# Gated recurrent mixer of a three-layer kernel: the order of scores, wide slabs, gate slabs and state rounds, and which engine splits the wide slabs

## The chip, the cores and the metric

The kernel runs on one core of a Trainium2 chip. The metric is device time in microseconds (us), the median of three runs. TensorE, VectorE (DVE), ScalarE (ACT), GpSimd (POOL) and the DMA queue of SyncE (SP) each run an instruction stream of their own; semaphores order them.

## The reference, cut to what matters

Three layers follow each other: a pooling and retention mixer, a gated recurrent mixer (`mixer_c`, stage "c" of the kernel) and a state space mixer, each followed by a routed expert layer ("peer"). The change is in stage c alone. There are 256 tokens of width 1024, eight heads of 128, and chunks of 32 tokens:

```python
def hgrn2_chunkwise(q, k, v, logf):
    b = jnp.cumsum(lc, axis=3)                     # within a chunk of 32
    b_last = b[:, :, :, -1:, :]
    q_in = qc * jnp.exp(b)
    k_in = kc * jnp.exp(-b)
    k_out = kc * jnp.exp(b_last - b)
    scores = jnp.where(causal, jnp.einsum('nbhcd,nbhsd->nbhcs', q_in, k_in), 0.0)
    intra = jnp.einsum('nbhcs,nbhse->nbhce', scores, vc)
    chunk_decay = jnp.exp(b_last[:, :, :, 0, :])
    def step(state, inp):
        cross = jnp.einsum('bhcd,bhde->bhce', q_n, state)
        state = state * d_n[..., None] + jnp.einsum('bhsd,bhse->bhde', k_n, v_n)
        return state, cross

def mixer_c(x, w_in, lower_bound, norm_g, w_out):
    q, fz, i, g = jnp.split(x @ w_in, C_SPLITS, axis=-1)
    f = lower_bound + (1.0 - lower_bound) * jax.nn.sigmoid(fz)
    o = hgrn2_chunkwise(q, 1.0 - f, i, jnp.log(f))
    y = head_rmsnorm(o, norm_g) * jax.nn.silu(g)
    return y @ w_out
```

## The kernel before

All weights stream through a ring of three slots as slabs of 128 x 1024 fp32 (512 KB). A float32 product is made of three matmuls (lines 576 to 578) from two halves of each operand. So each slab passes four steps: SyncE's queue loads it into `ring` (line 375) when the split of the slab three before it is done; ScalarE copies it rounded to `w_hi` (line 829, a "lead") when TensorE has used the slab three before it; GpSimd, or in some stages VectorE, subtracts it to `w_lo` (line 527, `split_rest`, a "split"); TensorE multiplies. `hi`, `lo`, `used` and `evac` count these steps.

Stage c has 40 slabs, numbered here from 0. Slabs 0 to 15 are columns (24 matmuls each, one PSUM bank of 256 columns): the gate logits f of the eight heads, then q. Slabs 16 to 23 are the wide ones (12 matmuls of 512 columns each), which accumulate v over all eight slabs in the four `acc` banks. Slabs 24 to 31 are columns again, the output gate g. Slabs 32 to 39 are rows of the output matrix (12 matmuls each, accumulating in `acc`). A column's PSUM bank is emptied by ScalarE (`column`, line 836, counted by `evac`), which then leads the slab three further on.

Between them lies the recurrence. VectorE turns sigmoid(f) into f (line 1935) and 1 - f (line 1939); ScalarE takes the log of the halves (line 1856); VectorE does the cumulative sums, one scan for each head (line 1943); ScalarE takes exponentials (line 1860), VectorE multiplies them into keys and queries (lines 1951 to 1958). TensorE then makes the scores (line 1774, in `acc`, after v has been copied out at line 849), VectorE masks them into `probs` (line 1962), TensorE transposes the outgoing keys (line 1784, in `acc`), ScalarE copies them (line 1891). Then come four state rounds, for tile 0 and 1 of the tokens and four heads each: `outers` (line 1802) makes the additions to the state of three or four chunks, VectorE folds them into the states (lines 1992 and 1995), `cross` (line 1812) reads the states. `intra` (line 1791) multiplies scores and v. ScalarE squares each tile (line 1898), VectorE and ScalarE make 1/std and y (lines 1969 to 1976), TensorE transposes y (line 1836), VectorE multiplies by gain and gate (line 2006) and halves the result (`coef`, lines 1235 and 1237), and the row slabs follow.

TensorE's order before: slabs 0 to 23; gate slabs 0 and 1 (slabs 24, 25); scores; gate slabs 2 and 3; key transposes; gate slab 4; outers 0, intra 0, gate 5, outers 1, cross 0, gate 6, outers 2, cross 1, intra 1, gate 7, outers 3, cross 2, cross 3; transposes of y; the eight row slabs. GpSimd splits every slab of the stage. Orders are written out by hand for each engine; nothing is planned at run time.

## Time and profile before

| | |
|---|---|
| runs | 2933.29 us median (2929.36 to 2934.74) |
| profiled execution: own time / span | 2932.74 us / 2930.9 us |
| TensorE busy | 2875.5 us (98%) |
| VectorE / ScalarE / GpSimd busy | 1948.5 / 1559.9 / 923.8 us |
| mean granted TensorE clock | 0.996 of full |
| stage c on TensorE | from 911.68 to 1064.46 us of the span |

Times in rows are microseconds from the start of the span. A matmul's duration overlaps the next one, so the pace is read from the distance between starts. "PEclk" is the TensorE clock granted, as a share of 2.4 GHz.

### The profile page before, as it was taken

The page shows a single profiled execution, that of the slowest core. Times are in us where ns is not written, and L with a number is a line of the kernel's source. Part 1 is how long each engine was busy: PE and PEld are TensorE (multiplying, and loading weights), DVE is VectorE, ACT ScalarE, POOL GpSimd, SP SyncE. Part 2 cuts the span into 40 slices and gives each one's busy share as a digit, 9 for nine tenths or more (in the row PEclk, how much of TensorE's full clock was granted, in tenths as well). Part 3 has the DMA queues.
Part 4 walks back from the last instruction along what each step waited for, and adds up shares of the span by engine and source line. Part 5 has one row for each costly group of instructions (what it writes and reads, how often), then busy time and mean ns, then how long its engine had stood idle before and what let it go on. Part 6 is the DMA issues. An engine that isn't in the chain of part 4 may idle for free.

```text
span 2930.9 us, 59692 instructions
## 1 busy us (share of the span) xinstructions
PE 2875.5 (98%) x21515; PEld 2624.2 (90%) x21515; DVE 1948.5 (66%) x3366; ACT 1559.9 (53%) x2555; POOL 923.8 (32%) x369
## 2 busy tenths in 40 slices
PE   8999999999999999999999999999999999999999
PEld 7899999888888879999998888889799999988887
DVE  4388577787555635947778855675629657788655
ACT  4444444676555544454467755654544544577554
POOL 3689500000005757980000000255779820000000
PEclk9999999999999999999999999999999999999999
DMA  6566555555765446665555576433465655555665
GB/s 215 158 183 186 184 169 171 173 175 177 238 193 155 141 126 186 183 186 169 170 172 177 175 237 195 145 130 124 155 188 180 183 178 171 173 172 177 206 193 162
DMA packets 146464, 515.20 MB, mean 176 GB/s; under 512 B 17552, under 2 KB 18576, under 8 KB 146336
## 3 DMA queue, kind: packets, MB, share of 16 engines
q1 hardware_dynamic: 146336, 513.46, 55.9%
q8 instruction: 85, 1.39, 0.2%
q14 instruction: 43, 0.35, 0.0%
HBM read 509.20 MB, written 4.19 MB: 175 GB/s over the span
## 4 chain that ended last, share of the span: by engine, by line
PE 89%; DVE 4%; POOL 3%; issue 2%; ACT 2%; DMA 0%; SPq 0%; DVEq 0%; ACTq 0%; POOLq 0%
PE col L576 15%; PE col L578 15%; PE col L577 15%; PE acc L576 13%; PE acc L578 12%; PE acc L577 12%; POOL w_lo L527 3%; PE col L723 2%; PE acc L723 2%; PE acc L683 1%; ACT w_hi L829 0%; ACT work L888 0%; PE acc L2211 0%; DVE work L2400 0%; PE misc L2224 0%
## 5 line engine op out<-in xcount | busy, mean ns | idle before, releaser
L527 POOL TENSOR_TENSOR w_lo<-ring,w_hi 128x1024 fp32r<-128x1024 f32 x365 | 923.6, 2541 | 1440.3 <-ACT w_hi L829 1439.9
L829 ACT ACTIVATE w_hi<-ring 128x1024 fp32r<-128x1024 f32 x941 | 993.4, 1056 | 538.1 <-PE acc L578 447.1
L576 PE MATMUL col<-x_hi,w_hi 128*128 128x256 f32 (+1 forms) x3976 | 1126.9, 283 | 12.0 <-POOL w_lo L527 6.2
L577 PE MATMUL col<-x_lo,w_hi 128*128 128x256 f32 (+1 forms) x3976 | 1120.5, 282 | 0.0
L578 PE MATMUL col<-x_hi,w_lo 128*128 128x256 f32 (+1 forms) x3976 | 1120.0, 282 | 0.0
L527 DVE TENSOR_TENSOR w_lo<-ring,w_hi 128x1024 fp32r<-128x1024 f32 x576 | 704.2, 1223 | 371.3 <-ACT w_hi L829 367.9
L576 PEld LDWEIGHTS col<-x_hi,w_hi 128*128 128x128 f32 x3976 | 752.3, 189 | 17.0 <-issue 11.0
L578 PEld LDWEIGHTS col<-x_hi,w_lo 128*128 128x128 f32 x3976 | 753.3, 189 | 0.0
L577 PEld LDWEIGHTS col<-x_lo,w_hi 128*128 128x128 f32 x3976 | 749.2, 188 | 0.7
L576 PE MATMUL acc<-w_hi,c_hi 128*128 128x512 f32 x1664 | 654.6, 393 | 4.7 <-POOL w_lo L527 2.1
L578 PE MATMUL acc<-w_hi,c_lo 128*128 128x512 f32 x1664 | 648.8, 390 | 0.0
L577 PE MATMUL acc<-w_lo,c_hi 128*128 128x512 f32 x1664 | 648.0, 389 | 0.0
L836 ACT ACTIVATE work<-col 128x256 f32 (+1 forms) x464 | 178.8, 385 | 732.5 <-PE col L578 732.5
L576 PEld LDWEIGHTS acc<-w_hi,c_hi 128*128 128x128 f32 x1664 | 312.9, 188 | 70.0 <-issue 4.3
L578 PEld LDWEIGHTS acc<-w_hi,c_lo 128*128 128x128 f32 x1664 | 312.7, 188 | 66.1
L577 PEld LDWEIGHTS acc<-w_lo,c_hi 128*128 128x128 f32 x1664 | 313.1, 188 | 63.3
L1244 DVE TENSOR_TENSOR c_lo<-work,c_hi 128x256 fp32r<-128x256 f32 x390 | 165.2, 424 | 14.3 <-ACT c_hi L993 14.1
L993 ACT ACTIVATE c_hi<-work 128x256 fp32r (+1 forms) x384 | 153.6, 401 | 0.0
L1251 DVE MAX8 work<-work 128x8 f32<-128x128 f32 (+1 forms) x144 | 35.4, 322 | 168.0 <-ACT work L950 167.7
L1377 DVE SCALAR_TENSOR_TENSOR work<-acc,work 128x512 f32 (+1 forms) x96 | 61.8, 686 | 102.7 <-PE acc L723 102.7
L1366 DVE TENSOR_TENSOR h_tok<-mask_i,pairs_of_gate 128x2048 f16<-128x2048 f16 x96 | 123.6, 1287 | 0.0
L998 ACT ACTIVATE h_tok<-iota_fp,neg_i 128x128 f16<-128x128 f16 x384 | 121.8, 388 | 0.2
(294 smaller groups left out, 1890.1 us busy)
## 6 DMA issues: line engine op xcount, KB each, us to landing
ring<-in_u SPq DMA_DIRECT2D x384, 512.0 KB, 3.6
ring<-in_v SPq DMA_DIRECT2D x384, 512.0 KB, 3.6
ring<-in_wq SPq DMA_DIRECT2D x48, 512.0 KB, 3.6
ring<-in_s_in SPq DMA_DIRECT2D x21, 512.0 KB, 3.2
ring<-in_c_in SPq DMA_DIRECT2D x16, 512.0 KB, 4.1
ring<-in_s_out SPq DMA_DIRECT2D x16, 512.0 KB, 3.2
ring<-in_s_gate SPq DMA_DIRECT2D x12, 512.0 KB, 3.2
ring<-in_s_conv SPq DMA_DIRECT2D x12, 512.0 KB, 3.2
```

The costliest lines, as they stand in the source:

```text
L527: eng.tensor_tensor(k.w_lo[s.slot][:, :], k.ring[s.slot][:, :], k.w_hi[s.slot][:, :].bitcast(F32), ALU.subtract).then_inc(k.lo[s.slot], 1)
L576: pe.matmul(out, a[0], b[0], start=start, stop=False, **kw)
L577: pe.matmul(out, a[0], b[1], start=False, stop=False, **kw)
L578: return pe.matmul(out, a[1], b[0], start=False, stop=stop, **kw)
L723: ins = pe.matmul(banks[t // HALF][:, t % HALF * EARLY:(t % HALF + 1) * EARLY], k.oh1[:, t, :], k.oh2[:, n, t, :], start=n == 0, stop=n == ...
L829: act.activation(k.w_hi[s.slot][:, :], k.ring[s.slot][:, :], ACT.Copy).then_inc(k.hi[s.slot], 1)
L836: act.activation(dst, src, func).then_inc(k.evac, 1)
L993: act.activation(k.c_hi[s.slot][:, :], act_of[:, s.index(values), :], ACT.Copy).then_inc(k.coef_h, 1)
L998: act.activation(k.oh1[:, t, :], k.iota_b[:, :], ACT.Abs, bias=k.neg_i1[:, at])\
L1244: dve.tensor_tensor(k.c_lo[s.slot][:, :], src, k.c_hi[s.slot][:, :].bitcast(F32), ALU.subtract).then_inc(k.coef[s.slot], 1)
L1366: dve.tensor_tensor(k.oh2.rearrange("p n t (i two) -> p n t i two", two=2), mask.unsqueeze(1).to_broadcast(shape), k.gate[:, bass.ds(b.ind ...
L1377: ins = dve.scalar_tensor_tensor(part, banks[half][:, :].rearrange("p (t i) -> p i t", t=HALF), 1.0 / GATE_UNIT, part, ALU.mult, ALU.mult)
```

## The change

Five things change, all in stage c.

1. VectorE, not GpSimd, splits the eight wide slabs; its stream has one `split` between other steps for each. GpSimd goes from slab 15 straight to slab 24.
2. The recurrence's front part is cut into halves of four heads: f, 1 - f, log, scans, exponentials and products. The f of a head is made as soon as its column is out. The clearing of `probs` is moved behind the small chain on the lower bound, and ScalarE leads slab 3 ahead of its first sigmoid.
3. The scores are made between wide slabs 19 and 20 and no longer use `acc`: `spare` is the three column banks and `misc`. The key transposes follow slab 23, in the same banks.
4. Gate slabs 0 and 1 follow the key transposes, 2 to 5 stand in the state rounds, 6 and 7 behind the first six transposes of y of each tile. `outers` 0 waits for the copies of gate slabs 0 and 1. Gates use one bank, but for gate 1.
5. Squares, and the signal for them, go by round and not by tile; the root of each tile stands between Silu copies on ScalarE. The last transposes of y (heads 6 and 7) follow the first row slab.

```diff
                 part = f"{name}_{part}"
-                if part == "ab_wide":
+                if part in ("ab_wide", "c_wide"):
                     continue
                 if k.first[part]:
                     stage(part, k.count[part])
...
-    def column(self, s, dst, func=ACT.Copy, n=T, src=None):
+    def column(self, s, dst, func=ACT.Copy, n=T, src=None, lead=True):
...
         act.activation(dst, src, func).then_inc(k.evac, 1)
-        self.split_lead(s + self.AHEAD)
+        if lead:
+            self.split_lead(s + self.AHEAD)
...
-        self.banks = [*k.col, k.misc]
+        gate = k.first["c_gate"]
+        self.spare = [*(k.col[(gate + n) % SLOTS] for n in range(SLOTS)), k.misc]
...
     def outer_banks(self, t):
-        k, gate = self.k, self.k.first["c_gate"]
-        spare = [k.col[(gate + n) % SLOTS] for n in (3, 4)]
-        return [k.misc, spare[0], *([k.acc[2], k.acc[3]] if t == 0 else [spare[1]])]
+        k, (_, near, far, misc) = self.k, self.spare
+        return [misc, near, *([k.acc[2], k.acc[3]] if t == 0 else [far])]
     def gate_bank(self, n):
-        return self.k.col[(self.k.first["c_gate"] + min(n, 5)) % SLOTS]
+        return self.spare[n == 1]
+
+    def y_bank(self, h):
+
+        near, far, misc = self.spare[1:]
+        return (near, far, misc, self.spare[0])[h // 2]
...
-        for c in range(DC):
-            e.wide(Slab(first + 16 + c), c, k.acc)
-
-        def gate_slabs(*ns):
-            for n in ns:
-                if n > 5:
-                    pe.wait_ge(k.evac, k.cols_before[first + 24 + n])
-                e.features(Slab(first + 24 + n), bank=self.gate_bank(n))
-
-        gate_slabs(0, 1)
-        w.next(m["c_wide"], 4)
-        w.next(m["c_qk"])
+
+        def wide(*chunks):
+            for c in chunks:
+                e.wide(Slab(first + 16 + c), c, k.acc)
+
+        def gate_slab(n):
+            if n > 1:
+                pe.wait_ge(k.evac, k.cols_before[first + 24 + n])
+            e.features(Slab(first + 24 + n), bank=self.gate_bank(n))
+
+        wide(0, 1, 2, 3)
+        pe.wait_ge(k.evac, k.cols_before[first + 16])
+        w.next(m["c_qk"], 2)
         for t in range(NT):
             for h in range(CH):
                 cut = slice(t * P, (t + 1) * P)
-                ins = pe.matmul(self.block(k.acc, t, h), self.f[:, h, cut], self.q[:, h, cut],
+                ins = pe.matmul(self.block(self.spare, t, h), self.f[:, h, cut], self.q[:, h, cut],
                                 start=True, stop=True)
                 if h % 4 == 3:
                     ins.then_inc(m["c_scores"], 1)
-        gate_slabs(2, 3)
+        wide(4, 5, 6, 7)
         w.next(m["c_probs"], 4)
-        w.next(m["c_kout"])
+        w.next(m["c_kout"], 2)
         for t in range(NT):
             for h in range(CH):
-                ins = pe.transpose(self.block(k.acc, t, h), self.b[:, h, t * P:(t + 1) * P], k.ident[:, :])
+                ins = pe.transpose(self.block(self.spare, t, h), self.b[:, h, t * P:(t + 1) * P], k.ident[:, :])
                 if h % 4 == 3:
                     ins.then_inc(m["c_koutT"], 1)
-        gate_slabs(4)
+        for n in range(2):
+            w.next(m["c_ktok"])
+            gate_slab(n)
...
                 pe.wait_ge(m["c_state"], self.states_before(group))
-            pe.wait_ge(k.evac, k.cols_before[first + 28 + t])
+            else:
+                pe.wait_ge(k.evac, k.cols_before[first + 26])
...
+
+        def transposes(t, heads):
+            for h in heads:
+                ins = pe.transpose(self.y_bank(h)[:, h % 2 * T + t * P:h % 2 * T + (t + 1) * P],
+                                   self.y[:, t, h * P:(h + 1) * P], k.ident[:, :])
+                if t and h % 2:
+                    ins.then_inc(m["c_yT"], 1)
+
+        w.next(m["c_wide"], 4)
+        w.next(m["c_ktok"], 2)
         outers(0)
         intra(0)
-        gate_slabs(5)
+        gate_slab(2)
         outers(1)
         cross(0)
-        gate_slabs(6)
+        gate_slab(3)
         outers(2)
         cross(1)
         intra(1)
-        gate_slabs(7)
+        gate_slab(4)
         outers(3)
         cross(2)
+        gate_slab(5)
         cross(3)
+        for t in range(NT):
+            w.next(m["c_y"])
+            transposes(t, range(4))
+            w.next(m["c_y"])
+            transposes(t, range(4, 6))
+            gate_slab(6 + t)
+        e.row_stage("c_out", 8, 0, 1)
         pe.wait_ge(k.evac, k.cols_before[first + 32])
         for t in range(NT):
-            for half in range(2):
-                w.next(m["c_y"])
-                for h in range(4 * half, 4 * half + 4):
-                    ins = pe.transpose(self.banks[h // 2][:, h % 2 * T + t * P:h % 2 * T + (t + 1) * P],
-                                       self.y[:, t, h * P:(h + 1) * P], k.ident[:, :])
-                    if t and h % 2:
-                        ins.then_inc(m["c_yT"], 1)
-        e.row_stage("c_out", 8)
+            transposes(t, range(6, 8))
+        e.row_stage("c_out", 8, 1)
...
         def log(half):
-            if half == 0:
-                w.next(m["c_f"])
+            w.next(m["c_f"])
...
+        w.next(m["c_lb"])
+        act.activation(self.exps, self.exps, ACT.Exp).then_inc(m["c_lbe"], 1)
+        e.leads(first, 1)
+        for n in range(8):
+            e.column(Slab(first + n), self.f[:, n, :], ACT.Sigmoid, lead=n > 0)
+        log(0)
         for n in range(8):
             e.column(Slab(first + 8 + n), self.q[:, n, :])
-            if n in (3, 4):
-                log(n - 3)
-        for n in range(DC):
+            if n == 0:
+                log(1)
+            if n == 5:
+                w.next(m["c_b"])
+                exp(self.f, 0, "c_exps", -1.0)
+            if n == 6:
+                exp(self.log, 0, "c_exps")
+        w.next(m["c_b"])
+        exp(self.f, 1, "c_exps", -1.0)
+        exp(self.log, 1, "c_exps")
+        for n in range(DC - 1):
             e.leads(first + 16 + n, 1)
-            if n == 2:
-                w.next(m["c_b"])
-                for half in range(2):
-                    exp(self.f, half, "c_exps", -1.0)
-            if n == 3:
-                for half in range(2):
-                    exp(self.log, half, "c_exps")
-            if n == 6:
+            if n in (2, 3):
                 w.next(m["c_diff"])
-                for half in range(2):
-                    exp(self.b, half, "c_expdiff")
-        e.wide(first + 16 + DC - 1, [(k.acc[t * 2 + half], self.v[:, t, half * 512:(half + 1) * 512], ACT.Copy)
-                                     for t in range(NT) for half in range(2)], m["c_wide"])
+                exp(self.b, n - 2, "c_expdiff")
+
+        def ktok(b):
+            w.next(m["c_koutT"])
+            t, h = divmod(4 * b, CH)
+            act.activation(self.ktok[:, t, h:h + 4, :], self.spare[b][:, :].rearrange("p (h d) -> p h d", h=4), ACT.Copy)\
+               .then_inc(m["c_ktok"], 1)
...
-        def squares(t):
+        def squares(group):
+            t, half = self.GROUPS[group]
             w.next(m["c_out"])
-            for h in range(CH):
+            for h in range(4 * half, 4 * half + 4):
                 n = t * CH + h
...
-        gates(4, 5, 6)
+        ktok(0)
+        e.leads(first + 16 + DC - 1, 1)
+        for b in range(1, 4):
+            ktok(b)
+        e.wide(first + 16 + DC - 1, [(k.acc[t * 2 + half], self.v[:, t, half * 512:(half + 1) * 512], ACT.Copy)
+                                     for t in range(NT) for half in range(2)], m["c_wide"])
+        gates(0, 1, 2)
         squares(0)
-        gates(7)
+        gates(3)
+        squares(1)
         std(0)
-        squares(1)
+        gates(4)
+        squares(2)
+        gates(5)
+        squares(3)
         std(1)
+        gates(6, 7)
     def vector(self, e):
         k, dve, w, own = self.k, e.dve, e.w, e.own
         m = k.m
         before = k.cols_before[k.first["c_in"]]
+        halves = (slice(0, CH // 2), slice(CH // 2, CH))
         w.next(k.mload[1], 16 * self.CONSTS)
         own.do(dve.tensor_tensor(self.max, self.bound[:, 0, :], self.bound[:, 1, :], ALU.max))
-        own.do(dve.memset(self.probs, 0.0))
         own.join()
         dve.tensor_tensor(self.exps, self.bound, self.max.unsqueeze(1).to_broadcast([P, 2, CH]), ALU.subtract)\
            .then_inc(m["c_lb"], 1)
...
-        w.next(m["c_f"])
-        own.do(dve.tensor_scalar(self.key, self.f, -1.0, 1.0, ALU.mult, ALU.add))
...
+        for half in halves:
+            for h in range(half.start, half.stop):
+                dve.wait_ge(k.evac, before + h + 1)
+                ins = dve.tensor_scalar(self.f[:, h, :], self.f[:, h, :], self.span[:, h:h + 1],
+                                        self.low[:, h:h + 1], ALU.mult, ALU.add)
+            ins.then_inc(m["c_f"], 1)
+            w.next(m["c_f"])
+            own.do(dve.tensor_scalar(self.key[:, half, :], self.f[:, half, :], -1.0, 1.0, ALU.mult, ALU.add))
...
-        w.next(m["c_exps"], 2)
-        own.do(dve.tensor_tensor(self.f, self.f, self.key, ALU.mult))
-        w.next(m["c_exps"], 2)
-        dve.tensor_tensor(by_chunk, last.unsqueeze(2).to_broadcast([P, CH * T // CCH, CCH]), by_chunk, ALU.subtract)\
-           .then_inc(m["c_diff"], 1)
-        dve.wait_ge(k.evac, before + 16)
-        dve.tensor_tensor(self.q, self.q, self.log, ALU.mult).then_inc(m["c_qk"], 1)
-        w.next(m["c_expdiff"], 2)
...
+
+        def split(*chunks):
+            for c in chunks:
+                split_rest(k, dve, Slab(k.first["c_wide"] + c))
+
+        def scans(*hs):
+            for h in hs:
+                ins = dve.tensor_tensor_scan(self.b[:, h, :], self.restart, self.log[:, h, :], 0.0, ALU.mult, ALU.add)
+            return ins
+
+        def chunk_ends(half):
+            w.next(m["c_b"])
+            cut = slice(half * per_half, (half + 1) * per_half)
+            own.do(dve.tensor_copy(last[:, cut], by_chunk[:, cut, CCH - 1]))
+
+        def keys_in(half):
+            w.next(m["c_exps"])
+            own.do(dve.tensor_tensor(self.f[:, halves[half], :], self.f[:, halves[half], :],
+                                     self.key[:, halves[half], :], ALU.mult))
+
+        def queries(half):
+            w.next(m["c_exps"])
+            dve.wait_ge(k.evac, before + 12 + 4 * half)
+            own.join()
+            dve.tensor_tensor(self.q[:, halves[half], :], self.q[:, halves[half], :],
+                              self.log[:, halves[half], :], ALU.mult).then_inc(m["c_qk"], 1)
+
+        def differences(half):
+            cut = slice(half * per_half, (half + 1) * per_half)
+            dve.tensor_tensor(by_chunk[:, cut, :], last[:, cut].unsqueeze(2).to_broadcast([P, per_half, CCH]),
+                              by_chunk[:, cut, :], ALU.subtract).then_inc(m["c_diff"], 1)
+
+        def keys_out(half):
+            w.next(m["c_expdiff"])
+            dve.tensor_tensor(self.b[:, halves[half], :], self.b[:, halves[half], :],
+                              self.key[:, halves[half], :], ALU.mult).then_inc(m["c_kout"], 1)
+
+        def probs(b):
             w.next(m["c_scores"])
             t, h = divmod(4 * b, CH)
             dve.copy_predicated(self.probs[:, t, h:h + 4, :], self.causal.unsqueeze(1).to_broadcast([P, 4, P]),
-                                k.acc[b][:, :].rearrange("p (h c) -> p h c", h=4)).then_inc(m["c_probs"], 1)
+                                self.spare[b][:, :].rearrange("p (h c) -> p h c", h=4)).then_inc(m["c_probs"], 1)
+
+        w.next(m["c_logf"])
+        scans(0, 1, 2, 3).then_inc(m["c_b"], 1)
+        chunk_ends(0)
+        w.next(m["c_logf"])
+        scans(4)
+        split(0)
+        scans(5, 6, 7).then_inc(m["c_b"], 1)
+        chunk_ends(1)
+        split(1)
+        keys_in(0)
+        split(2)
+        queries(0)
+        split(3)
+        keys_in(1)
+        queries(1)
+        split(4)
+        differences(0)
+        differences(1)
+        split(5)
+        split(6)
+        keys_out(0)
+        keys_out(1)
+        probs(0)
+        probs(1)
+        split(7)
+        probs(2)
+        probs(3)
         def finish(t):
             cut = slice(t * CH, (t + 1) * CH)
-            w.next(m["c_msq"])
+            w.next(m["c_msq"], 2)
             dve.tensor_scalar(self.var[:, cut], self.msq[:, cut], 1.0 / P, LN_EPS, ALU.mult, ALU.add)\
                .then_inc(k.var, 1)
             w.next(k.std)
...
                 ins.then_inc(m["c_y"], 1)
...
+
+        for group in range(3):
+            states(group)
         finish(0)
+        states(3)
         finish(1)
-        first = k.first["c_out"]
-        dve.wait_ge(k.evac, k.cols_before[first])
+        out, gate = k.first["c_out"], k.first["c_gate"]
         for n in range(8):
             if n % 2 == 0:
                 w.next(m["c_yT"])
-            yT = self.banks[n // 2][:, n % 2 * T:(n % 2 + 1) * T]
+            dve.wait_ge(k.evac, k.cols_before[gate + n + 1])
+            yT = self.y_bank(n)[:, n % 2 * T:(n % 2 + 1) * T]
             own.do(dve.scalar_tensor_tensor(yT, yT, self.gain[:, n:n + 1], self.g[:, n, :], ALU.mult, ALU.mult))
             own.join()
-            e.coef(yT, Slab(first + n))
```

## Rows read from the trace of the kernel before

**Rows 1.** Windows of stage c: length, busy PE, PEld, DVE, ACT, POOL, clock, DMA.
```profile
960.00:989.20 29.20, 23.89 (x97) 18.47 (x95) 25.94 (x11) 16.14 (x17) 24.80 (x9) 0.94 0.44 144
...
1034.30:1044.60 10.30, 8.25 (x41) 6.26 (x30) 7.01 (x16) 2.39 (x17) 0.00 (x0) 0.50 0.11 45
```

**Rows 2.** Timeline of TensorE: start, duration, engine, line, tiles, count, idle before.
```profile
911.68 0.36 PE L576 MATMUL col<-x_hi,w_hi 128*128 128x256 f32 x1 [0.85 <-DVE x_lo L1088]
...
922.73 0.36 PE L576 MATMUL col<-x_hi,w_hi 128*128 128x256 f32 x1 [2.29 <-POOL w_lo L527]
...
959.69 0.39 PE L576 MATMUL acc<-w_hi,x_hi 128*128 128x512 f32 x1
...
976.09 0.39 PE L578 MATMUL acc<-w_hi,x_lo 128*128 128x512 f32 x1
...
980.28 0.80 PE L576 MATMUL acc<-w_hi,x_hi 128*128 128x512 f32 x1 [3.80 <-POOL w_lo L527]
...
989.16 0.36 PE L576 MATMUL col<-x_hi,w_hi 128*128 128x256 f32 x1 [1.45 <-POOL w_lo L527]
...
993.54 0.36 PE L576 MATMUL col<-x_hi,w_hi 128*128 128x256 f32 x1 [1.30 <-POOL w_lo L527]
...
1021.95 0.37 PE L1802 MATMUL misc<-work 32*128 32x128 f32 x1 [0.46 <-DVE work L1992]
...
1033.59 1.29 PE L1812 MATMUL acc<-work 128*32 128x128 f32 x32 [2.54 <-DVE work L1992]
...
1040.83 0.79 PE L576 MATMUL acc<-w_hi,c_hi 128*128 128x512 f32 x1 [0.29 <-DVE c_lo L1237]
...
1064.46 1.48 PE L633 MATMUL col<-ident 128*128 128x256 bf16 x12
```

**Rows 3.** Timeline of ScalarE around its first Exp and a table load.
```profile
917.30 0.22 ACT L1847 ACTIVATE work<-work 128x16 f32<-128x16 f32 x1 [3.59 <-DVE work L1922]
...
949.88 1.28 ACT L1856 ACT_TABLE_LOAD   x1
951.17 1.06 ACT L1856 ACTIVATE work<-work 128x1024 f32<-128x1024 f32 x1
```

**Rows 4.** Timelines of GpSimd and VectorE where both work from SBUF.
```profile
912.50 2.41 POOL L527 TENSOR_TENSOR w_lo<-ring,w_hi 128x1024 fp32r<-128x1024 f32 x1 [1.70 <-ACT w_hi L829]
...
912.65 2.27 DVE L1919 TENSOR_TENSOR work<-work 128x8 f32<-128x8 f32 x1
...
915.30 1.76 DVE L1920 MEMSET work<- 128x2048 f32 x1 [0.38 <-issue]
...
970.18 3.40 DVE L1943 TENSOR_TENSOR_SCAN work<-work 128x256 f32<-128x256 f32 x2
...
975.72 2.29 DVE L1951 TENSOR_TENSOR work<-work 128x2048 f32<-128x2048 f32 x1 [1.88 <-ACT work L1860]
...
978.49 3.88 DVE L1953 TENSOR_TENSOR work<-work 128x2048 f32<-128x2048 f32 x1 [0.48 <-ACT work L1860]
...
976.65 3.58 POOL L527 TENSOR_TENSOR w_lo<-ring,w_hi 128x1024 fp32r<-128x1024 f32 x1 [4.20 <-ACT w_hi L829]
```

**Rows 5.** Groups by line, on VectorE: split over the whole span, scans in stage c.
```profile
L527 DVE TENSOR_TENSOR w_lo<-ring,w_hi 128x1024 fp32r<-128x1024 f32 x576 | 704.2, 1223 | 371.3 <-ACT w_hi L829 367.9
...
L1943 DVE TENSOR_TENSOR_SCAN work<-work 128x256 f32<-128x256 f32 x8 | 19.1, 2461 | 6.3 <-ACT work L1856 6.3
```

**Rows 6.** Groups by line on ScalarE in stage c: column, square, value copies.
```profile
L836 ACT ACTIVATE work<-col 128x256 f32<-128x256 f32 x24 | 9.2, 383 | 38.7 <-PE col L578 38.7
...
L1898 ACT ACTIVATE work<-acc 128x128 f32<-128x128 f32 x16 | 4.2, 291 | 2.4 <-PE acc L1812 2.4
...
L849 ACT ACTIVATE work<-acc 128x512 f32<-128x512 f32 x4 | 2.0, 596 | 0.0
```

**Rows 7.** Timeline of VectorE in a state round, two chunks of four heads.
```profile
1013.68 2.28 DVE L1992 SCALAR_TENSOR_TENSOR work<-work,acc 128x128 f32<-128x128 f32 x8
```

**Rows 8.** DMA issues of the wide slabs: count, size, us to landing.
```profile
ring<-in_c_wide SPq DMA_DIRECT2D x8, 512.0 KB, 3.6
```

37 lines of the change are left out of this document (8 added, 29 removed).

## The prediction

> **What bounds the kernel now.** I read the windows of stage c first, then TensorE's timeline, then the two engines that split slabs. TensorE is busy for 98% of the span, and stage c is passed from its first matmul at 911.68 to the next stage's first at 1064.46, 152.8 us [rows 2]. Nothing but TensorE's end of the stage starts what follows it, so what TensorE loses there is lost in full. The windows show two poor stretches: 960 to 989.2, where TensorE does 23.9 us in 29.2, and 1034.3 to 1044.6, where its granted clock is 0.50, that is 1.2 GHz [rows 1].
>
> From the timeline [rows 2] I sum what the stage loses:
>
> - Start: slab 3 begins at 922.73 and the slabs before it end at 920.28: 2.45 us.
> - A column slab takes 2.84 us (13 of them from 922.73 to 959.69). A wide one takes 2.77 us (71 distances from 959.69 to 976.09 are 0.231 us each, times 12). Eight are 22.2 us, but from the first wide slab to the first gate slab at 989.16 pass 29.5: 7.3 us lost. In it are 3.80 idle before 980.28, a half clock behind that wait (the first matmul lasts 0.80), and 1.45 idle.
> - Gate slab 0 to gate slab 1: 4.38 us for 2.84: 1.5 us.
> - The state rounds: 0.46 us before `outers` 2.
> - The end: the wait for the last states begins at 1031.05 (1033.59 less 2.54), the row slabs at 1040.83. In these 9.8 us lie 32 small matmuls (1.0 to 1.3 us) and 16 transposes, which at half clock take some 3.8 and would take 1.9. Some 6.9 us are lost.
> - The first row slab runs at half clock from 1040.83 to 1044.6 [rows 1, 2]: half of 3.8, 1.9 us.
>
> Together 20.6 us. The named releaser of the first four waits is GpSimd's `w_lo`.
>
> **Why GpSimd is late.** Its own work on a slab is 2.4 us, below TensorE's 2.77. But it and VectorE lock each other out. VectorE's product of 8 elements at 912.65 takes 2.27 us and ends at 914.92, just when GpSimd's split of 912.50 ends. The product of 2048 elements takes 2.29 us alone at 975.72 and 3.88 at 978.49, from where GpSimd's split of 976.65 still runs to 980.23; that one in turn began inside the first product and took 3.58 [rows 4]. The scans tell it best: their mean is 2.46 us [rows 5], but the last two together take 3.40, one behind a GpSimd split (2.75) and one with GpSimd idle, 0.66 [rows 4]. So I price a scan at 0.66 of its own, plus at most one split if GpSimd is busy, and a product of 1024 elements at half of 2.29, 1.15.
>
> The Trainium skill (SBUF — State Buffer, Who interferes with whom) has the same rule: an exclusive lock of the shared port pair for a whole instruction, taken also by VectorE instructions with two SBUF inputs. It speaks against moving a split to VectorE, as that has two such inputs; the rows agree, and the cost would be 1.2 us per split for GpSimd. Here it costs nothing while GpSimd has no slab.
>
> **The change, part by part.**
>
> *Start.* The Exp at 917.30 waited 3.59 us for VectorE, 1.76 of it and 0.38 before it for the clearing of `probs` [rows 3, 4]. Moved behind, Exp runs at about 915.5. ScalarE's copy of slab 3 (1.06) follows at once, before the Sigmoid table (1.28), and GpSimd has the slab at about 919.2; it is needed at 920.2. The 2.45 us go. Slab 4 is ready at about 922, needed at 923.
>
> *Wide slabs.* Slab 16 then starts at 920.2 + 13 x 2.84 = 957.1, slab 17 at 959.9. Log and scans come earlier: ScalarE's copy of a column (0.38 [rows 6]) and VectorE's 0.4 behind a split put f of the last head at 936.3 the first log at 938.2. Scans 0 to 3 each slip between two GpSimd splits, one per 2.94 us, and end at 948.6. GpSimd so needs 2.4 + 0.6 = 3.0 per slab against 2.84, for four slabs; it has 0.8 us in hand there and keeps 0.4. Slab 15, its last, ends at 953.5. From then to about 978, when slab 24 is copied, GpSimd is idle. VectorE does scan 4, the split of slab 16 (1.22 [rows 5]) by 955.2, three scans at 0.6, the split of slab 17 by 958.4: 1.5 us before it is due. Then a product and a split alternate, 2.4 us per slab against 2.77: slabs 18, 19, 20 at 960.6, 962.8, 966.2, needed at 962.6, 965.4 and 971.5. The query products end at 965.0, the scores start at 968.1, so they cost only their own 3.5 us, as before. The ring's loads follow VectorE's splits now; 3.6 us to landing [rows 8] from 955.2 is 959, and ScalarE wants slab 19 at 960.5. Covered. The 7.3 and the 1.5 us go. If the cover fails, a late split costs its lateness once, and above some 2.5 us a half clock too, as at 980.28.
>
> *Behind the wide slabs a new wait.* `outers` 0 now waits until gate slabs 0 and 1 are copied. From the end of slab 23 ScalarE needs 0.65 for the first quarter of transposes, then four key copies (2.0), a lead (0.95), four value copies (2.0), the Silu table (1.28 [rows 3]), gate 0 (0.27), a lead (0.95) and gate 1 (0.38 [rows 6]): 8.4 us. TensorE has transposes (1.66) and two gates (5.68): 7.3. It waits 1.1 us; behind it queue all rounds.
>
> *Rounds.* Each chunk is 1.14 us on VectorE [rows 7], a group of four 4.3 with its 0.9 of copies. Between `outers` 1 and 2 TensorE has 3.8 of work: 0.8 wait (before 0.46). Gate 5 (2.84) now covers the last states' 2.54 wait. Gate 6 covers y of tile 1, mostly: from `cross` 3 squares 1.1 (four at 0.29 [rows 6], read out between), root with its own table load 1.28 and small steps, y 0.7 are some 4.1; TensorE has the first transposes and gate 6, 3.5: 0.5 wait. Gate 7 covers the first `coef`. So the 6.9 us go, but for this.
>
> *Table loads.* Three more Silu/Sqrt switches and one at the end of the stage, 1.3 each on ScalarE [rows 3]; two lie in the waits above, the others beside TensorE. The Trainium skill (ScalarE: Activation LUTs, What ACT_TABLE_LOAD costs) adds a drain of about 1.38 us for each switch. In rows 3 the next instruction starts 1.29 us after the load does. By the page both waits would be some 1.4 us longer, and the time 2.8 us longer.
>
> *Clock.* After waits of 1.45 and 1.30 us the first matmul took 0.36, that is full clock; after 3.80 it took 0.80, and after 2.54 half clock began [rows 1, 2]. The new waits are at most 1.1, so I expect full clock and the 1.9 back. Bounds: nothing, or the 10.3 us at half that stand there now, which cost 5.
>
> **Sum.** 20.6 lost before, 1.1 + 0.8 + 0.5 = 2.4 lost after: 18.2 us less. The profiled execution had 2932.74, so 2914.6; the median of the runs is 0.55 above it: 2915.1, rounded to 2915.
>
> **Rivals.**
>
> 1. *Clock falls in the rounds anyhow.* They are made of small matmuls, and it fell among them at 1034. The two stays at half in this stage last some 3 and 10.3 us [rows 1, 2] and so cost 1.5 and 5: 2917 to 2920. Against it: gates stand between all rounds now. 12%.
> 2. *Scans cost more with GpSimd idle*, about 2.8 each as most did before. Then slab 17 is ready at 963, 3.1 us late, half a clock dip follows: 2919. Only the one scan of 0.66 speaks against it, but clearly. 7%.
> 3. *The group's mean is the scan's own price, with the lock held.* GpSimd then needs 4.9 us per slab: four slabs 2 us late each, and 5.5 more at slabs 17 and 18: 2928, no measurable change. 3%.
> 4. *A table switch holds ScalarE for more than its load.* If it cost twice the 1.29 us between the starts there, as it might where much is in flight, the waits before `outers` 0 and for y would be 1.3 longer each: 2918. Against it, nothing of the kind stands in [rows 3]. 6%. (The page on the Activation LUTs in the Trainium skill, named above, says about that.)
> 5. *Slower.* TensorE's clock stays at half from `outers` 0 on through the rounds and row slabs, because waits of 1.1, 0.8 and 0.5 follow each other. Half clock costs half the time spent in it; to eat 18 us it must last 36 us. Its longest stay in stage c is 10.3 us [rows 1]. All 55 us that remain would be doubled: up to 2970. 2%.
>
> The forecast itself has 70%, with its own range 2911 to 2919 (no new wait at all: 2.4 less; a clock dip at another stage border, of which a shift of 18 us can make or take one: 1.7 either way). Cases 1, 2 and 4 lie below 2920. The range 2910 to 2920.5 leaves out rivals 3 and 5 and the tails. A change of 0.2% (5.9 us) is about what a measurement of this kernel can tell from none. Faster has 94%, same 4% (case 3 and a mixture), slower 2%.
>
> **What would show it.** Right: TensorE from slab 0 to the next stage in about 134.5 us; slab 3 without a wait; no GpSimd split between slabs 15 and 24; scans 5 to 7 in under 2.2 us; three waits of 1.1, 0.8 and 0.5 us; granted clock 1.00 throughout. Wrong: a wait of TensorE on VectorE's `w_lo` at slab 17 or 18, column slabs 12 to 15 late by GpSimd, or a stretch at 0.50 in the rounds.

## The result: 2912.6 us, 20 us faster, and the profile after

The changed kernel takes 2912.62 us (median of 6 runs, 2912.00 to 2914.78) beside 2932.86 us for the kernel before on the same chip (6 runs, 2929.36 to 2936.62). The ratio is 0.9926, with a 95% interval from 0.9916 to 0.9937. The forecast was 2915.0 us, with a range from 2910 to 2920.5.

In the profiled execution (span 2910.7 us, before 2930.9) stage c goes from TensorE's first matmul at 911.11 to the next stage's first at 1046.05: 134.94 us, where 152.8 stood and 134.5 was expected. The stage gives 17.8 of the 20.2 us of span. The other 2.4 lie outside the edits (0.6 ahead of the stage, 1.8 behind). Span less stage c was 2778.1 us before and 2775.8 after, and over all profiled executions of this study it lay between 2775.6 and 2780.2 whatever the edit. The 2.4 us lie within that scatter, so below I compare the length of stage c, from one profiled execution of each kernel. The changed kernel profiled a second time had 134.71 us; 0.2 us is thus what two executions of one kernel showed.

The page's first part, busy time, share of the span and count for each engine:

```profile
PE 2868.4 (99%) x21515; PEld 2619.3 (90%) x21515; DVE 1940.5 (67%) x3380; ACT 1566.0 (54%) x2559; POOL 896.2 (31%) x361
```

TensorE's busy time fell by 7 us and its span by 20: most of what went was idle time. GpSimd's fell by 27.6 us, all of it in stage c (103.3 to 75.8), where eight splits at 2.4 are 19.2: the other 8.4 are splits that no longer run beside VectorE.

The windows come next. The first spans the same time as the first of [rows 1], the second the end of the rounds and the first row slab. Columns as there.

```profile
960.00:989.20 29.20, 29.20 (x173) 25.57 (x172) 17.64 (x18) 17.03 (x21) 7.19 (x3) 1.00 0.55 168
1014.00:1025.00 11.00, 10.54 (x106) 9.62 (x106) 7.18 (x16) 7.50 (x17) 4.79 (x2) 1.00 0.35 98
```

The 29.2 us that held 23.9 of matmuls are full, and GpSimd (last of the pairs) fell from 24.80 to 7.19. At the end of the rounds the granted clock is 1.00 where 0.50 stood.

TensorE's timeline, in the lines that answer to [rows 2]:

```profile
967.89 2.84 PE L1781 MATMUL col<-work 128*128 128x128 f32 x24
...
982.58 1.48 PE L1791 MATMUL col<-ident,work 128*128 128x128 f32 x12
...
991.24 0.34 PE L1812 MATMUL misc<-work 32*128 32x128 f32 x1 [1.11 <-ACT work L836]
...
1002.83 0.37 PE L1812 MATMUL misc<-work 32*128 32x128 f32 x1 [0.46 <-DVE work L2074]
...
1020.06 0.65 PE L1828 MATMUL col<-ident,work 128*128 128x128 f32 x4 [0.46 <-DVE work L2057]
...
1023.77 0.39 PE L576 MATMUL acc<-w_hi,c_hi 128*128 128x512 f32 x1
```

The brackets are all the waits above 0.3 us in the stage: before `outers` 0, before `outers` 2 and before the transposes of y of tile 1. They sum to 2.0 us. Scores (L1781) and key transposes (L1791) start without one, and the first row slab's matmul lasts 0.39, full clock, where [rows 2] show 0.79.

VectorE and GpSimd between slab 10 and slab 24:

```profile
938.31 4.60 DVE L1982 TENSOR_TENSOR_SCAN work<-work 128x256 f32<-128x256 f32 x4 [2.36 <-ACT work L1869]
942.95 2.21 DVE L1988 COPY work<-work 128x32 f32<-128x32 f32 x1
...
954.22 1.23 DVE L527 TENSOR_TENSOR w_lo<-ring,w_hi 128x1024 fp32r<-128x1024 f32 x1 [8.46 <-ACT w_hi L829]
955.36 1.85 DVE L1982 TENSOR_TENSOR_SCAN work<-work 128x256 f32<-128x256 f32 x3
957.25 0.19 DVE L1988 COPY work<-work 128x32 f32<-128x32 f32 x1
957.81 1.23 DVE L527 TENSOR_TENSOR w_lo<-ring,w_hi 128x1024 fp32r<-128x1024 f32 x1 [0.37 <-ACT w_hi L829]
...
939.51 13.16 POOL L527 TENSOR_TENSOR w_lo<-ring,w_hi 128x1024 fp32r<-128x1024 f32 x5 [1.20 <-ACT w_hi L829]
978.37 2.40 POOL L527 TENSOR_TENSOR w_lo<-ring,w_hi 128x1024 fp32r<-128x1024 f32 x1 [25.70 <-ACT w_hi L829]
```

Each pair of numbers is start and duration. The three scans behind 955.36 have GpSimd idle and take 1.85 together. Of the first four, the last waits for GpSimd's split of 939.51, which ends at 942.37; the small copy of chunk ends takes 2.21 beside GpSimd and 0.19 without it. From 952.67 to 978.37 GpSimd has nothing.

### The profile page after: what moved, and what is told of

Its sections match the earlier page's. It is cut to its first block, busy times and chain, and to the rows that moved or that the text cites. A ratio compares the mean times of both kernels' runs of the same rounds, so it can differ in the third digit from the quotient of the medians.

```text
span 2910.7 us, 59696 instructions
## 1 busy us (share of the span) xinstructions
PE 2868.4 (99%) x21515; PEld 2619.3 (90%) x21515; DVE 1940.5 (67%) x3380; ACT 1566.0 (54%) x2559; POOL 896.2 (31%) x361
## 3 DMA queue, kind: packets, MB, share of 16 engines
q8 instruction: 85, 1.39, 0.2%
## 4 chain that ended last, share of the span: by engine, by line
PE 91%; DVE 3%; POOL 2%; issue 2%; ACT 2%; DMA 0%; SPq 0%; DVEq 0%; ACTq 0%; POOLq 0%
PE col L576 15%; PE col L578 15%; PE col L577 15%; PE acc L576 13%; PE acc L578 13%; PE acc L577 13%; POOL w_lo L527 2%; PE col L723 2%; PE acc L723 2%; PE acc L683 1%; DVE work L2486 0%; ACT work L889 0%; ACT w_hi L829 0%; PE acc L2297 0%; PE misc L2310 0%
## 5 line engine op out<-in xcount | busy, mean ns | idle before, releaser
L527 POOL TENSOR_TENSOR w_lo<-ring,w_hi 128x1024 fp32r<-128x1024 f32 x357 | 896.0, 2520 | 1448.3 <-ACT w_hi L829 1447.3
L527 DVE TENSOR_TENSOR w_lo<-ring,w_hi 128x1024 fp32r<-128x1024 f32 x584 | 714.1, 1223 | 378.6 <-ACT w_hi L829 375.6
```

The source lines that it names most:

```text
L527: eng.tensor_tensor(k.w_lo[s.slot][:, :], k.ring[s.slot][:, :], k.w_hi[s.slot][:, :].bitcast(F32), ALU.subtract).then_inc(k.lo[s.slot], 1)
```

## Experiments

Twelve runs follow, one of them the changed kernel itself. Each is told with the length of stage c, against 134.94 us (after) or 152.78 us (before); ratios are to the kernel before on the same chip.

### The whole forecast: the changed kernel again

> The changed kernel once more, unchanged, as the measure for the three kernels beside it on this chip. Every theory expects stage c at 134.9 us from its first matmul to the next stage's, as in the first execution (134.94), and a ratio of 0.993 to the kernel before. How far this stage length comes out from 134.94 says how far such a length may be trusted: within 0.3 us if it is as good a measure as I take it for; if it differs by 1 us or more, the differences of 1 to 2 us read from the other runs mean little.

Stage c was 134.71 us, the median 2913.08, the ratio 0.9926 [0.9912, 0.9939]. By this one repeat, differences of 1 us in the stage can be read.

### Who splits the wide slabs

GpSimd splits them again, all else as after:

```diff
-                if part in ("ab_wide", "c_wide"):
+                if part == "ab_wide":
                     continue
...
         def split(*chunks):
-            for c in chunks:
-                split_rest(k, dve, Slab(k.first["c_wide"] + c))
+            pass
```

> The changed kernel, but GpSimd splits the eight wide slabs again and VectorE splits none; all else stays. Theory (each locks the other out of SBUF for a whole instruction): VectorE's scans and its products now run among GpSimd's splits again, the splits of slabs 16 to 22 take 3 to 3.6 us each where VectorE works beside them, TensorE waits for w_lo once or more in the wide slabs, 3 to 6 us in all, and stage c is about 4.6 us longer than the changed kernel's 134.9. Rival (GpSimd's 2.4 us per split is below TensorE's 2.77, and cutting the recurrence into halves was what helped): no wait, within 1 us of the changed kernel.

Stage c was 136.89 us, 1.95 more; ratio 0.9933 [0.9916, 0.995]. That lies between the two theories, and the waits are elsewhere than mine had them:

```profile
968.20 0.51 PE L576 MATMUL acc<-w_hi,x_hi 128*128 128x512 f32 x1 [0.19 <-POOL w_lo L527]
...
972.71 2.92 PE L1781 MATMUL col<-work 128*128 128x128 f32 x24 [1.47 <-DVE work L1998]
```

`w_lo` costs almost nothing. TensorE waits for the query products (L1998 there), which with their neighbours take 3.2 to 3.4 us each beside GpSimd and not 1.22. GpSimd's own five splits behind 959.01 take 15.76 us, 3.15 each where TensorE takes 2.77, but TensorE never waited for it by more than 0.2.

The opposite: VectorE splits, and GpSimd is kept busy by six subtractions of its own, so that it locks VectorE out as before.

```diff
+                if part == "c_wide":
+                    room = [view(k.big, NORMED + n * D, D) for n in range(3)]
+                    for n in range(6):
+                        pool.tensor_tensor(room[0], room[1], room[2], ALU.subtract).then_inc(k.extra, 1)
+                        pool.wait_ge(k.extra, n + 1)
                 if part in ("ab_wide", "c_wide"):
                     continue
```

> The changed kernel, and GpSimd does six more subtractions of 128 x 1024 from SBUF behind slab 15, whose result nobody reads. TensorE, ScalarE and the semaphores between the engines are as they were. Theory (lock): each of VectorE's scans 5 to 7, its splits and its products waits for one such subtraction, so that its stream falls back by up to 2.4 us at each step for some 20 us; TensorE waits for slab 17 or 18, 8 to 13 us in all. Rival (the engines share SBUF freely, a scan is slow for another reason): scans stay at 0.66 us, TensorE's time does not change.

Stage c was 146.41 us (910.97 to 1057.38), 11.5 more; the ratio 0.9968 [0.9956, 0.9981]. My theory said 8 to 13. The timelines of GpSimd, VectorE and TensorE:

```profile
952.75 18.25 POOL L562 TENSOR_TENSOR work<-work 128x1024 f32<-128x1024 f32 x6
...
953.80 8.32 DVE L1988 TENSOR_TENSOR_SCAN work<-work 128x256 f32<-128x256 f32 x3
...
964.25 1.21 DVE L528 TENSOR_TENSOR w_lo<-ring,w_hi 128x1024 fp32r<-128x1024 f32 x1
...
965.51 0.79 PE L582 MATMUL acc<-w_hi,x_hi 128*128 128x512 f32 x1 [6.07 <-DVE w_lo L528]
```

The same three scans take 8.32 us, 2.77 each, and not 1.85 in all. Slab 17 is 6.07 us late, the clock falls in that wait, and TensorE waits 1.89 more for slab 18. The six subtractions share no buffer with VectorE's instructions; what is left between them is the lock.

### The same split in the order of before

```diff
-                if part == "ab_wide":
+                if part in ("ab_wide", "c_wide"):
                     continue
...
             ins = dve.tensor_tensor_scan(self.b[:, h, :], self.restart, self.log[:, h, :], 0.0, ALU.mult, ALU.add)
+            if h in (0, 3, 5):
+                split((0, 3, 5).index(h))
...
+        split(3)
         w.next(m["c_exps"], 2)
         own.do(dve.tensor_tensor(self.f, self.f, self.key, ALU.mult))
+        split(4)
```

(and 5 to 7 between the later products of the kernel before.)

> The kernel before, with one part of the change alone: VectorE splits the wide slabs, between the uncut scans and products. Theory: the mutual waits of the two engines go, but the scans still begin at 954 and the wide slabs are bound to the exponentials on ScalarE and the products of 2048; TensorE still waits some 5 us at slab 20, and the time is 2 to 5 us less than before, far from the whole. Rival (moving the split is the whole of the gain up to the gates): 7 to 9 us less than before.

Stage c was 151.70 us, 1.1 less than before; ratio 0.999 [0.998, 0.9999]. The medians differ by 3.3 us (2931.09 and 2934.40), inside the 2 to 5 of my theory, but only 1.1 of that lies in the stage. The eight scans take 6.4 us in all where they took 19.1 [rows 5], and yet (timelines of VectorE and TensorE):

```profile
972.16 2.29 DVE L1957 TENSOR_TENSOR work<-work 128x2048 f32<-128x2048 f32 x1 [7.16 <-ACT work L1860]
974.37 1.22 DVE L527 TENSOR_TENSOR w_lo<-ring,w_hi 128x1024 fp32r<-128x1024 f32 x1
...
975.64 0.80 PE L576 MATMUL acc<-w_hi,x_hi 128*128 128x512 f32 x1 [5.18 <-DVE w_lo L527]
```

The split of slab 20 is queued behind a product, the product waits 7.16 us for ScalarE's exponentials, and these stand behind ScalarE's copy of slab 21, which waits for TensorE. The wait of 3.80 in [rows 2] became one of 5.18.

With this run the two orders and the two engines are all there. Stage c, and in it TensorE's time for the eight wide slabs with the waits among and right behind them (from start to start, without the scores):

| | GpSimd splits | VectorE splits |
|---|---|---|
| order of before | 152.78, of it 29.47 | 151.70, of it 29.31 |
| order of after | 136.89, of it 24.40 | 134.94, of it 22.31 |

The engine is worth 0.2 us at the wide slabs in the old order and 2.1 in the new one; the order is worth 5.1 and 7.0. So I tested the place of the exponentials on the changed kernel:

```diff
         for n in range(8):
             e.column(Slab(first + 8 + n), self.q[:, n, :])
...
-            if n == 5:
-                w.next(m["c_b"])
-                exp(self.f, 0, "c_exps", -1.0)
-            if n == 6:
-                exp(self.log, 0, "c_exps")
-        w.next(m["c_b"])
-        exp(self.f, 1, "c_exps", -1.0)
-        exp(self.log, 1, "c_exps")
         for n in range(DC - 1):
             e.leads(first + 16 + n, 1)
+            if n == 0:
+                for half in range(2):
+                    w.next(m["c_b"])
+                    exp(self.f, half, "c_exps", -1.0)
+                    exp(self.log, half, "c_exps")
```

> On the changed kernel ScalarE makes the four exponentials of both halves only behind the 16 columns and the copy of slab 19, where the kernel before had them among the wide slabs. VectorE's stream is unchanged, and it still has the splits. My theory after the run in which the old order got VectorE's splits and gained only 1.1 us: the early exponentials by halves, and not the engine that splits, carry most of the 7.3 us at the wide slabs, because VectorE's splits are queued behind products that wait for them. The exponentials then end from 963.3 us on, the product of the first half at 964.6, the split of slab 18 at 965.8, due at 962.4: 3.4 us late, and with half a clock behind it 3.5 to 5 us more in stage c: 138.4 to 140. Rival: the engine that splits is what matters, and the place of the exponentials costs within 1 us: 135 to 136.

Stage c was 139.62 us, 4.7 more (2919.23 us, ratio 0.9946 [0.993, 0.9961]). VectorE and TensorE:

```profile
963.31 1.23 DVE L1989 TENSOR_TENSOR work<-work 128x1024 f32<-128x1024 f32 x1 [6.14 <-ACT work L1873]
964.45 1.22 DVE L527 TENSOR_TENSOR w_lo<-ring,w_hi 128x1024 fp32r<-128x1024 f32 x1
...
965.73 0.50 PE L576 MATMUL acc<-w_hi,x_hi 128*128 128x512 f32 x1 [3.12 <-DVE w_lo L527]
```

3.12 us of wait and a stretch at half clock of 3.4 us from 966.7 on, worth 1.7, make 4.8, beside the measured 4.7. Early exponentials are worth more here than the engine that splits. Early logs are not:

```diff
-        log(0)
         for n in range(8):
             e.column(Slab(first + 8 + n), self.q[:, n, :])
-            if n == 0:
-                log(1)
+            if n in (3, 4):
+                log(n - 3)
```

> On the changed kernel ScalarE takes the two logs behind q columns 3 and 4, where the kernel before had them, instead of ahead of the q columns and behind the first. The exponentials keep their new place. Theory: GpSimd is idle from 952.7 us on, so the scans that begin at about 949.5 run at 0.66 us each but for one or two that wait for a GpSimd split; the split of slab 17 is ready about when it is due (0.5 us of slack in the changed kernel), and the first exponentials end 1.2 us later. Stage c is longer by 0 to 1 us. Rival: the early scans are what makes room, as eight scans among GpSimd's splits would take 2.8 us each: 3 us or more.

Stage c was 134.70 us, no change (2915.78 us, ratio 0.9933 [0.9917, 0.9948]). The scans ran from 952.42 to 960.75 of that trace, whose stage began 3.2 us later, and the splits still came in time.

### The start, the scores, gate slab 5

Three undo one placement each. The start (clearing of `probs` ahead of the chain, slab 3 copied behind the first sigmoid):

```diff
-        e.leads(first, 1)
         for n in range(8):
-            e.column(Slab(first + n), self.f[:, n, :], ACT.Sigmoid, lead=n > 0)
+            e.column(Slab(first + n), self.f[:, n, :], ACT.Sigmoid)
...
+        own.do(dve.memset(self.probs, 0.0))
         own.join()
...
-        own.do(dve.memset(self.probs, 0.0))
         own.join()
```

> The changed kernel with the start as it was before: probs cleared ahead of the small chain, slab 3 led behind the first sigmoid. Theory: TensorE waits 2.3 to 2.5 us for slab 3 and the whole is longer by that. Rival (the later stages have slack that takes it up): below 1 us.

Stage c was 137.28 us, 2.3 more (ratio 0.9952 [0.9937, 0.9968]). The wait is back as it was in [rows 2], and at full clock behind it:

```profile
923.56 0.35 PE L576 MATMUL col<-x_hi,w_hi 128*128 128x256 f32 x1 [2.29 <-POOL w_lo L527]
```

The scores moved behind slab 23 (`probs` 0 and 1 then follow the last split):

```diff
-        wide(0, 1, 2, 3)
+        wide(0, 1, 2, 3, 4, 5, 6, 7)
...
-        wide(4, 5, 6, 7)
```

> The changed kernel, with the scores behind wide slab 23 and not between 19 and 20; VectorE's last split moves ahead of the masks to fit. Theory: only the masks are uncovered then, TensorE waits about 1 us for them before the key transposes: 1 us longer. Rival (the scores' place is a main part of the gain): 3.5 us or more.

Stage c was 136.00 us, 1.1 more, 0.82 of it one wait of the key transposes for VectorE's masks. Among the wide slabs the masks are covered.

Gate slab 5 behind the last `cross`:

```diff
         cross(2)
-        gate_slab(5)
         cross(3)
+        gate_slab(5)
```

> The changed kernel, with gate slab 5 behind cross 3 and not before it. Theory: TensorE waits some 2.7 us for the states of the last round, as before the change, and y of tile 1 comes later by as much as ScalarE's squares wait for gate 5: 3 to 4 us longer than the changed kernel, and 1.5 to 2 more if the clock falls behind the wait. Rival (gate 5 covers nothing, since y of tile 1 ends last anyway): within 0.5 us.

Stage c was 141.18 us, 6.2 more (2919.15 us, ratio 0.9945 [0.993, 0.996]). My theory had the mechanism; the size is just above the 6 us that its upper ends add up to:

```profile
1014.32 1.93 PE L1822 MATMUL acc<-work 128*32 128x128 f32 x32 [2.54 <-DVE work L2074]
...
1026.33 0.66 PE L1828 MATMUL col<-ident,work 128*128 128x128 f32 x4 [1.54 <-DVE work L2057]
```

The window of the half clock, columns as in [rows 1]:

```profile
1013.70:1020.50 6.80, 6.18 (x52) 5.70 (x53) 0.56 (x3) 0.00 (x0) 0.00 (x0) 0.50 0.22 80
```

The wait of 2.54 is that of [rows 2] to the digit, the clock falls with it for 6.8 us, and the wait for y of tile 1 grows from 0.46 to 1.54. From start to start, `cross` 3 with its wait takes 3.46 us longer than in the changed kernel, gate slab 5 at half clock 1.85, and gate slab 6 with the wait behind it 1.1.

### Feeding TensorE through the wait, in the kernel before

```diff
         cross(2)
+        pe.wait_ge(k.evac, k.cols_before[first + 32])
+        ones = k.ident[:, :].bitcast(BF16)
+        for _ in range(20):
+            pe.matmul(self.gate_bank(7)[:, 0:2 * P], ones[:, 0:P], ones, start=True, stop=True)
         cross(3)
```

Twenty matmuls, whose results nothing reads, fill the 2.54 us. Their operands, called `ones` here, are the identity tile read as bf16.

> The kernel before, with 20 small matmuls of ones into a free bank between cross 2 and cross 3, where TensorE stood idle for 2.54 us. They hide no wait. Theory (the clock fell because TensorE stood idle there): the wait becomes work, the granted clock stays at full from 1034 to 1044, and the transposes of y and the first row slab gain 1.9 us each: 3 to 4 us less than before. Rival (the small matmuls of the rounds bring the clock down, or the later waits of 1.67 us do): half clock stays, 0 to 0.5 us.

My theory failed. Stage c was 152.73 us, the time 2933.52, ratio 0.9996 [0.9986, 1.0005]:

```profile
1030.30 2.36 PE L1833 MATMUL col<-ident 128*128 128x256 bf16 x20
1032.90 1.08 PE L1812 MATMUL acc<-work 128*32 128x128 f32 x32 [0.25 <-DVE work L1996]
1034.28 0.94 PE L1840 MATMUL col<-ident,work 128*128 128x128 f32 x6 [0.29 <-DVE work L1980]
...
1037.69 1.54 PE L1840 MATMUL col<-ident,work 128*128 128x128 f32 x6 [2.25 <-DVE work L1980]
```

`cross` 3 ran at full clock (1.08 us, not 1.29). The next wait, for y of tile 1, grew from 1.67 to 2.25, the clock fell there, and the row slabs began as late as ever (128.98 us behind the start of the stage, 129.15 before). The half clock up to the second transposes costs nothing while VectorE and ScalarE set the end of the chain. That the filling kept the clock up isn't shown either. The kernel before with VectorE's splits, told above, had nothing in that wait, and yet:

```profile
1031.34 1.08 PE L1812 MATMUL acc<-work 128*32 128x128 f32 x32 [2.54 <-DVE work L2002]
...
1036.12 1.04 PE L1836 MATMUL col<-ident,work 128*128 128x128 f32 x6 [2.24 <-DVE work L1986]
...
1038.13 0.79 PE L576 MATMUL acc<-w_hi,c_hi 128*128 128x512 f32 x1 [0.75 <-DVE c_lo L1237]
```

`cross` 3 takes the same 1.08 us behind an empty wait of 2.54, the granted clock is 1.00 from 1031 to 1037, and it is 0.50 only behind the next wait. The changed kernel puts gates 5 and 6, work that has to be done anyway, into the two waits; no run filled the second alone.

### Below the changed kernel

Gate slab 1 in the third bank, so that `outers` 0 waits for no copy:

```diff
-        return self.spare[n == 1]
+        return self.spare[2 * (n == 1)]
...
-            else:
-                pe.wait_ge(k.evac, k.cols_before[first + 26])
```

(The waits of gate slab 1 and of `outers` 0 for the key copies are shifted to fit.)

> The changed kernel, with gate slab 1 in the third column bank, which outers of tile 0 do not use, so that outers 0 waits no more for the copies of gate slabs 0 and 1. Theory: the wait of 1.11 us goes and nothing takes its place: 1.1 us less. Rival (the value copies of ScalarE, which outers 0 needs too, end last): no change.

Stage c was 133.63 us, 1.3 less: the wait before `outers` 0 is gone, the other two stay at 0.46. The ratio of 0.9932 [0.9918, 0.9945] doesn't tell it from the changed kernel's; that profiled execution began its stage c 3.3 us later, behind a half-clock stretch of 6.8 us at 63 us of the span. With it, a second edit:

```diff
         squares(3)
         std(1)
+        e.leads(first + 29, 1)
         gates(6, 7)
```

(and gate 5's own lead left out), so that GpSimd splits nothing while VectorE makes the root of tile 1.

> Two edits on the changed kernel. Gate slab 1 lies in the third bank of the key transposes instead of the second, so that outers 0 waits for no copy of a gate, and ScalarE's copy of the slab three behind gate slab 5 is made behind the root of tile 1 instead of ahead of the squares. My theory: the first takes away the wait of 1.1 us before outers 0 (stage c was 133.63 us with it alone), the second takes away GpSimd's split that ran while VectorE's 8-element step on var waited (1.43 us instead of 0.2), and with it the 0.46 us before the transposes of y of tile 1; the later copy is hidden behind gate slab 6. Stage c at 133.2 us, 1.7 less than the changed kernel and 0.4 less than with the first edit alone; medians 1.5 to 2 us below the changed kernel's on this chip. Rival: the step on var isn't what the transposes wait for, or the later copy makes a gate slab late: stage c at 133.6 or above.

The rival was right on the sum: 134.17 us, 0.5 more than with the first edit alone, and 2913.46 us beside 2913.08 for the changed kernel on that chip, which is no difference. The step on the variance got short as I had said (first line), but that was hardly what the transposes had waited for:

```profile
1016.10 0.17 DVE L2050 TENSOR_SCALAR work<-work 128x8 f32<-128x8 f32 x1 [2.78 <-ACT work L1914]
1017.62 0.20 DVE L2053 RECIPROCAL work<-work 128x8 f32<-128x8 f32 x1 [1.35 <-ACT work L872]
...
1020.29 0.39 PE L576 MATMUL col<-x_hi,w_hi 128*128 128x256 f32 x1 [0.64 <-ACT work L836]
```

The 8-element step took 0.17 us and not 1.43, and the transposes no longer waited. But the next step on VectorE waits for ScalarE's root, whose table load of 1.28 us runs meanwhile: from the start of the 8-element step to the reciprocal pass 1.52 us here and 1.70 in the changed kernel. So the lock had cost 0.18 us there. Another 0.2 came from the squares: they begin 1.14 us behind `cross` 3 and not 1.34, as the copy of the slab no longer stands ahead of them. That copy now stands ahead of ScalarE's copy of gate slab 6, so gate slab 7 waits 0.64 us for its bank.

## Why the prediction was right, step by step

- *Start.* First Exp at 914.59 (said 915.5), slab 3 split at 918.5 (919.2), no wait. The 2.45 us went; the undo gave 2.3 back. Shown.
- *Wide slabs, the 7.3 and 1.5 us.* They went, but the reason I gave was by itself the smaller part of it. The section on why GpSimd is late named the lock, and the lock is real (11.5 us with GpSimd kept busy). Yet with GpSimd splitting again only 1.95 us came back, with late exponentials 4.7, and VectorE's splits alone in the old order brought 1.1. So most was a queue, in an order of instructions. It was another queue in the kernel before than in the two runs that show splits behind products. There the split of slab 22, which TensorE waited 3.80 us for, had itself waited 4.20 for ScalarE's copy ([rows 4], at 976.65), and on ScalarE that copy stood behind exponentials that waited for the last scan:

```profile
973.61 2.01 ACT L1860 ACTIVATE work<-work 128x1024 f32<-128x1024 f32 x2 [2.49 <-DVE work L1943]
975.53 1.04 ACT L829 ACTIVATE w_hi<-ring 128x1024 fp32r<-128x1024 f32 x1
```

  The prediction reads past this 4.20. Its term came out because it was the whole loss of those slabs, whatever its cause, and because the new order was worked out slab by slab; it is no evidence for the lock. The lock's part in the kernel before is indirect too: it drew the eight scans out to 19.1 us, where they took 6.4 with VectorE splitting. The undos overlap and don't add up to 8.8; how the sum divides stays open.
- *Scans.* 0.66 with GpSimd idle: scans 5 to 7 took 1.85 together (said under 2.2). The group's mean fell from 2461 to 943 ns. Scans 0 to 3 took 4.60 in a row, not one per 2.94: GpSimd was between slabs until 939.51. The mean of [rows 5] was a price with the lock in it.
- *Slab 17.* Its split ended at 959.04, said 958.4, due at 959.56 (956.79 and 2.77): 0.5 us in hand and not 1.5. ScalarE's copy of slab 16 had waited 1.44 us for its load, a wait that is in no sentence of mine: I had checked the load of slab 19 only. It didn't reach TensorE.
- *Scores.* Query products end 966.55 (said 965.0), scores start 967.89 (968.1).
- *New waits.* 1.11, 0.46, 0.46 for 1.1, 0.8, 0.5. The middle one was mis-sized: it is the 0.46 of before, since nothing was added between `outers` 1 and 2. The third has the right size. The 8-element step on the variance took 1.43 us beside a GpSimd split, which I hadn't seen, but the table load ran beside it and the root waited only 0.19:

```profile
1018.84 0.21 ACT L872 ACTIVATE work<-work 128x8 f32<-128x8 f32 x1 [0.19 <-DVE work L2050]
```

- *Sum.* 134.94 for 134.5, with 0.4 us less of waits than said. The six losses add up to 20.51 and not 20.6; with 2.4 for the new waits that is 134.67, and with the waits as measured 134.30, so 0.64 is missing. From start to start on TensorE the columns gave back 2.33 of 2.45, the wide slabs 7.16 of 7.3, gates 0 and 1 1.39 of 1.5 and the row slabs 1.70 of 1.9; gates 2 to 7 took 0.22 more in all without their waits, and the end gave 7.06 for 6.9. The columns by themselves differ by 0.2 between the two executions of the changed kernel.
- *Clock.* No stretch at half in stage c: the granted clock is 1.00 throughout. That alone puts rivals 1 and 5 out for this order. With `cross` 3 uncovered the fall came back at the same wait of 2.54 us. But the prediction's "above some 2.5 us" is no rule: a wait of 2.54 was followed by full clock in the kernel before with VectorE's splits, one of 1.89 by half clock where GpSimd was kept busy. What makes it fall is open. The end's 6.9 and 1.9 us: the undo of gate 5 alone gave 6.2 back.
- *Rival 4, table switches.* The Silu table's load before gate 0 and the next instruction:

```profile
988.20 1.28 ACT L836 ACT_TABLE_LOAD   x1
989.49 0.38 ACT L836 ACTIVATE work<-col 128x256 f32<-128x256 f32 x1
```

1.29 us from start to start, with no gap ahead of the load (the value copies of 986.10 take 2.08), and the wait before `outers` 0 is 1.11. The drain of about 1.38 us that the Trainium skill (ScalarE: Activation LUTs, What ACT_TABLE_LOAD costs) adds doesn't show here; the measurement decides.
- *Rivals 2 and 3* fall with the scans.
- *Not tested.* No run undid the f of each head, the cut into halves by itself, gates 6 and 7 behind the first transposes, the squares by round or the late transposes of heads 6 and 7.

## What to carry to other kernels

A split or any due work queued in order behind a product inherits that product's wait: ask what each instruction ahead of it waits for before asking which engine is free. The mean of a group can be mostly another engine's lock (2461 and 943 ns for the same scan), so take an operation's price from an instance with its neighbour idle. And look at the wait of the copy or load that a late instruction needed, not only at its engine. Filling a wait of TensorE with matmuls that nobody needs gave nothing here, as the next wait in the chain grew; moving needed ones in did (6.2 us for gate slab 5).

## What the runs showed of the hardware

- The lock doesn't ask for size. VectorE's copy of 128 x 32 took 2.21 us beside GpSimd and 0.19 without; a step on 128 x 8 took 1.43 and 0.17, and the longer one ended at 1018.81, as GpSimd's split did (1016.39 and 2.39 us). GpSimd pays as well: its six subtractions took 3.04 us each beside VectorE, where a split of the same size takes 2.40 with VectorE idle (978.37 in the changed kernel).
- The length of a wait alone doesn't tell whether TensorE's clock falls. Full clock followed waits of 2.29 us (start, columns around it) and, in the kernel before with VectorE's splits, one of 2.54 before `cross` 3. Half clock followed waits of 2.54 at the same place in the kernel before, of 3.12 (slab 18), of 2.25 in the run that fed TensorE, and of 1.89 at slab 18 where GpSimd was kept busy, some 3 us behind another stretch at half.
- Five of the 14 profiled executions have a half-clock stretch near 63 us of the span, far ahead of every edit: where it lasted 6.8 us, stage c began at 914 and not 911. This scatter of 3 us can hide edits of 1 us from a median of five runs, but not from the length of the stage.
